# Decode attention of eight samples: three banks' worth of data taken out of a ring of four, and TensorE's work for a sample put in another order

## The reference, cut to what matters

```python
gate = einsum(q, mean of keys per block of 256)              # MoBA: top 3 blocks and the own one
o_a  = gathered_block_attn(q_a, k, v, idx, ..., 256)
ck = compress(k_cmp); cv = compress(v_cmp)                   # windows of 32, stride 16: gelu(flat @ w1 + b1) @ w2 + b2
p_cmp = softmax(q_b . ck);  o_cmp = p_cmp @ cv               # NSA, compressed branch
imp = p_cmp @ overlap;  idx = top_k(imp, 16)                 # which blocks of 64 the selected branch reads
o_sel = gathered_block_attn(q_b, k_sel, v_sel, idx, ..., 64)
o_win = window_attn(q_b, last 512 and own keys)
```

## Time and profile before

| | us |
|---|---|
| median of 3 runs (lowest, highest) | 1169.08 (1166.57, 1170.09) |
| the profiled execution, its own time | 1166.52 |
| its span, from first to last instruction | 1164.7 |
| TensorE busy in the span | 1017.6 (87%) |
| VectorE, ScalarE busy | 595.3, 486.9 |

### The profile page before, as it was taken

How to read it: one execution, slowest core, us unless ns; L and a number is a source line. 1 busy time by engine, 2 the same in 40 slices (tenths; PEclk the granted TensorE clock), 3 DMA queues, 4 the chain that set the end, 5 groups by cost and what they waited for, 6 DMA issues and landing times. The chain is left out here.

```text
span 1164.7 us, 25938 instructions
## 1 busy us (share of the span) xinstructions
PE 1017.6 (87%) x9553; PEld 890.4 (76%) x9553; DVE 595.3 (51%) x1304; ACT 486.9 (42%) x982; POOL 83.0 (7%) x59
## 2 busy tenths in 40 slices
PE   7789986775788989888888888879999799999997
PEld 3578874555585868677776767668998799999997
DVE  1500015523675756565665757568547764455433
ACT  3312224733263635445363636263443354443223
POOL 1143410000000000001010000000000000000000
PEclk9789995857899998999999999988999899999999
DMA  9787767318567475756666574556574164443501
GB/s 328 211 301 246 245 239 247 150 50 300 180 203 253 154 257 166 256 169 239 208 218 235 175 260 161 172 165 172 167 233 146 37 217 145 144 144 145 181 0 46
DMA packets 132533, 220.17 MB, mean 189 GB/s; under 512 B 20948, under 2 KB 76753, under 8 KB 127682
## 3 DMA queue, kind: packets, MB, share of 16 engines
q1 hardware_dynamic: 127586, 185.79, 48.4%
q0 software_dynamic: 4896, 33.68, 8.2%
HBM read 210.99 MB, written 12.58 MB: 192 GB/s over the span
## 5 line engine op out<-in xcount | busy, mean ns | idle before, releaser
L1240 PE MATMUL ps<-t_XT,t_slab 128*128 128x128 f32 x1024 | 162.2, 302 | 27.8 <-DVE t_cv L1842 15.6
L1240 PEld LDWEIGHTS ps<-t_XT,t_slab 128*128 128x128 f32 x1024 | 144.4, 214 | 45.4 <-ACT t_PTs L1530 20.6
L103 PE MATMUL ps<-b_uH,b_slabH 128*128 128x320 f32 x480 | 150.7, 314 | 8.8 <-DVE b_uL L2402 5.3
L104 PE MATMUL ps<-b_uL,b_slabH 128*128 128x320 f32 x480 | 150.1, 313 | 0.0
L105 PE MATMUL ps<-b_uH,b_slabL 128*128 128x320 f32 x480 | 149.2, 311 | 0.0
L2290 DVE TENSOR_TENSOR b_slabL<-t_slab,b_slabH 128x2048 fp32r<-128x2048 f32 (+1 forms) x52 | 109.3, 2125 | 64.1 <-ACT b_slabH L2183 64.0
L2183 ACT ACTIVATE b_slabH<-t_slab 128x2048 fp32r<-128x2048 f32 (+1 forms) x52 | 92.3, 1783 | 94.5 <-PE ps L105 87.2
L103 PEld LDWEIGHTS ps<-b_uH,b_slabH 128*128 128x128 f32 x480 | 91.8, 191 | 10.3 <-issue 6.6
L104 PEld LDWEIGHTS ps<-b_uL,b_slabH 128*128 128x128 f32 x480 | 91.8, 191 | 0.0
L105 PEld LDWEIGHTS ps<-b_uH,b_slabL 128*128 128x128 f32 x480 | 91.7, 191 | 0.0
L1240 PE MATMUL ps<-t_XT,t_taps 128*128 128x128 f32 x512 | 87.5, 287 | 0.0
(11 more groups left out here) (396 smaller groups left out, 2025.2 us busy)
## 6 DMA issues: line engine op xcount, KB each, us to landing
t_Kr<-cache_moba_kv SPq DMA_DIRECT2D x132, 256.0 KB, 3.0
t_Vr<-cache_moba_kv SPq DMA_DIRECT2D x124, 256.0 KB, 4.8
t_slab<-w_ada SPq DMA_DIRECT2D x22, 1024.0 KB, 7.9
t_slab<-w_gu SPq DMA_DIRECT2D x22, 1024.0 KB, 5.3
t_slab<-w_in SPq DMA_DIRECT2D x17, 1024.0 KB, 5.7
t_slab<-w_down SPq DMA_DIRECT2D x11, 1024.0 KB, 5.0
t_slab<-cmp_w SPq DMA_DIRECT2D x2, 2048.0 KB
t_wkv<-cache_nsa_win SPq DMA_DIRECT2D x8, 512.0 KB, 3.3
```

The costliest lines, as they stand in the source:

```text
L103: pe.matmul(out, w_high, x_high, start=start, stop=False, **kw)
L104: pe.matmul(out, w_high, x_low, start=False, stop=False, **kw)
L1240: return pe.matmul(out[:, P * j:P * j + P], taps(w, j, lp)[:, P * ht:P * ht + P], XT[:, w, lp, j, :, :].rearrange("p v i -> p (v i)"), sta ...
```

## The change

1. The window keys' transposes go to `S_WIN`, the transposes of `pwin` go to `H0`; both leave the ring (`OFF_RING`), and two empty places (`RESTS`) are put in so that the number of jobs on the ring stays a multiple of four. The compressed scores go to `H0` in place of `ps[7]`.
2. On TensorE `key_scores` becomes the last step of a sample, after `selected_scores(1)` and `hidden_keys(3)`. `moba_values(2)`, `segments(2)`, `compressed_values`, `selected_scores(0)`, `compressed_products` and `selected_transposes(2)` change places. At a sample's start 9 products (not 4) come ahead of `compressed_keys`, and 5 (not 8) between the window scores and the group sum.
3. On VectorE three of the four `gate_sums` come together ahead of `take_keys(0)`; the maximum of the compressed scores comes ahead of the additions to the own scores; the maximum of the window scores comes after that of the selected ones; the 16 `turn_keys` are spread otherwise.
4. On ScalarE the exponential of the window scores follows that of the selected ones; `relay_quarter(1)` comes ahead of the eight MoBA exponentials; quarter 1's work comes ahead of gelu, staging the queries after `relay_quarter(2)`, and the copy of quarter 2's selected keys after the output copy.

No arithmetic is added or removed, nor any transfer.

```diff
-STEADY = (FRONT_JOBS + cmp_jobs(0) + sel_jobs(0) + P_JOBS + cmp_jobs(1) + sel_jobs(1) + [("values", 0, 0), ("cout", 0, 0)]
-          + cmp_jobs(2) + sel_jobs(2) + cmp_jobs(3) + sel_jobs(3) + [("final", 0, 0)] + KEY_JOBS)
+RESTS = [("rest", 0, 0), ("rest", 1, 0)]
+OFF_RING = ("win", "pwin")
+STEADY = (FRONT_JOBS + RESTS + cmp_jobs(0) + sel_jobs(0) + P_JOBS + cmp_jobs(1) + sel_jobs(1)
+          + cmp_jobs(2) + [("values", 0, 0), ("cout", 0, 0)] + sel_jobs(2) + cmp_jobs(3) + sel_jobs(3) + [("final", 0, 0)] + KEY_JOBS)
...
+    def bank_of(it, job):
+
+        if job[0] in OFF_RING:
+            return S_WIN if job[0] == "win" else H0
+        return ps[RING[on_ring(NSA_JOBS if it is None else jobs_of(it)).index(job) % 4]]
...
             def sequence(it, more):
-                bank = ring(it, ("win", 0, 0))
+                bank = bank_of(it, ("win", 0, 0))
+                pe.wait_ge(scores_taken, it * N_SCORE + 2)
...
-                hidden_values(it, 0, range(0, 4), False)
+                hidden_values(it, 0, range(0, 9), False)
...
+                pe.matmul(H0[0:64, 0:NCMP], qb[:, :], ckT[:, 0:NCMP], start=True, stop=True).then_inc(small_mm, 1)
+                wait_emptied(it, ("win", 0, 0))
+                pe.matmul(S_WIN[0:64, :], qb[:, :], KTw[:, :], start=True, stop=True).then_inc(scored, 1)
+                hidden_values(it, 0, range(9, 14), False)
+                pe.wait_ge(pc_ready, it + 1)
                 pe.wait_ge(small_taken, it * 3 + 1)
-                pe.matmul(ps[7][0:64, 0:NCMP], qb[:, :], ckT[:, 0:NCMP], start=True, stop=True).then_inc(small_mm, 1)
-                wait_emptied(it, ("win", 0, 0))
-                pe.wait_ge(scores_taken, it * N_SCORE + 2)
-                pe.matmul(S_WIN[0:64, :], qb[:, :], KTw[:, :], start=True, stop=True).then_inc(scored, 1)
-                hidden_values(it, 0, range(4, 12), False)
-                pe.wait_ge(pc_ready, it + 1)
...
-                hidden_values(it, 0, range(12, 24), True)
+                hidden_values(it, 0, range(14, 24), True)
...
-                bank = ring(it, ("pwin", 0, 0))
+                bank = bank_of(it, ("pwin", 0, 0))
+                pe.wait_ge(exp_done, it * N_EXP + E_WIN)
...
+                moba_values(it, 2)
+                hidden_keys(it, it + 1, 1)
+                segments(2)
                 compressed_values(it)
-                hidden_keys(it, it + 1, 1)
+                selected_scores(it, it + 1, 0)
                 compressed_products(it)
-                moba_values(it, 2)
-                segments(2)
-                selected_scores(it, it + 1, 0)
-                selected_transposes(it, it + 1, 2)
                 hidden_keys(it, it + 1, 2)
                 moba_values(it, 3)
                 moba_own_values(it)
+                selected_transposes(it, it + 1, 2)
                 segments(3)
                 selected_transposes(it, it + 1, 3)
                 final_transposes(it)
-                key_scores(it, it + 1)
                 selected_scores(it, it + 1, 1)
                 hidden_keys(it, it + 1, 3)
+                key_scores(it, it + 1)
...
         def _(act):
...
                 act.wait_ge(max_done, it * N_MAX + 2)
-                exp(Sw[:, :], Sw[:, :], t["nmax"][:, 1:2], t["sums"][:, 1:2]).then_inc(exp_done, 1)
+                exp(Ss[:, :], Ss[:, :], t["sstat"][:, 0:1], t["sstat"][:, 1:2]).then_inc(exp_done, 1)
                 act.wait_ge(max_done, it * N_MAX + 3)
-                exp(Ss[:, :], Ss[:, :], t["sstat"][:, 0:1], t["sstat"][:, 1:2]).then_inc(exp_done, 1)
+                exp(Sw[:, :], Sw[:, :], t["nmax"][:, 1:2], t["sums"][:, 1:2]).then_inc(exp_done, 1)
...
                     odd_segments(it, 0, 1)
+                    relay_quarter(it, it + 1, 1)
...
-                if more:
-                    relay_quarter(it, it + 1, 1)
                 for q in (1, 3):
                     probability_copy(act, copy, it, q).then_inc(emptied_act, 1)
+                if more:
+                    keep_quarter(1)
+                    odd_segments(it, 1, 0)
+                    odd_segments(it, 1, 1)
+                    take_transposed_selected(it, 1)
                 act.wait_ge(hid_added, it * N_ADDED + 4)
                 gelu(1, 0)
                 gelu(1, 1).then_inc(cmp_act, 1)
                 if more:
+                    relay_quarter(it, it + 1, 2)
+                    keep_quarter(2)
                     stage_queries(it + 1)
                     pad_queries(it + 1)
-                    keep_quarter(1)
-                    odd_segments(it, 1, 0)
-                    odd_segments(it, 1, 1)
-                    take_transposed_selected(it, 1)
-                    relay_quarter(it, it + 1, 2)
-                    keep_quarter(2)
                     odd_segments(it, 2, 0)
                     odd_segments(it, 2, 1)
-                    take_transposed_selected(it, 2)
                     relay_quarter(it, it + 1, 3)
...
         def _(dve):
...
+                for i in range(3):
+                    gate_sums(it, i)
                 take_keys(it, 0)
-                dve.wait_ge(small_mm, it * N_SMALL + 1)
+                dve.wait_ge(small_mm, it * N_SMALL + 2)
+                dve.tensor_reduce(t["nmax"][:, 0:1], H0[0:64, 0:NCMP], AX.X, ALU.max, negate=True).then_inc(max_done, 1)
...
                 own_copy()
                 if more:
-                    turn_keys(it + 1, range(2, 6))
+                    turn_keys(it + 1, range(1, 4))
                     segment_differences(it, 1, 0)
                     segment_differences(it, 1, 1)
-                    values_copy()
-                    turn_keys(it + 1, range(6, 8))
-                    products_copy()
-                    turn_keys(it + 1, range(8, 12))
+                    turn_keys(it + 1, range(4, 8))
                     segment_differences(it, 2, 0)
                     segment_differences(it, 2, 1)
+                    values_copy()
                     take_selected(it + 1, 0)
-                    turn_keys(it + 1, range(12, 16))
+                    products_copy()
+                    turn_keys(it + 1, range(8, 14))
                     segment_differences(it, 3, 0)
                     segment_differences(it, 3, 1)
+                    turn_keys(it + 1, range(14, 16))
```

More of the change, by code:

```diff
@@ L983, with counted, on_ring @@
 P_JOBS = [("pmoba", q, 0) for q in range(4)] + [("pown", 0, 0)]
-STEADY = (FRONT_JOBS + cmp_jobs(0) + sel_jobs(0) + P_JOBS + cmp_jobs(1) + sel_jobs(1) + [("values", 0, 0), ("cout", 0, 0)]
-          + cmp_jobs(2) + sel_jobs(2) + cmp_jobs(3) + sel_jobs(3) + [("final", 0, 0)] + KEY_JOBS)
-LAST = FRONT_JOBS + P_JOBS + [("values", 0, 0), ("cout", 0, 0), ("final", 0, 0)]
+RESTS = [("rest", 0, 0), ("rest", 1, 0)]
+OFF_RING = ("win", "pwin")
+STEADY = (FRONT_JOBS + RESTS + cmp_jobs(0) + sel_jobs(0) + P_JOBS + cmp_jobs(1) + sel_jobs(1)
+          + cmp_jobs(2) + [("values", 0, 0), ("cout", 0, 0)] + sel_jobs(2) + cmp_jobs(3) + sel_jobs(3) + [("final", 0, 0)] + KEY_JOBS)
+LAST = FRONT_JOBS + RESTS + P_JOBS + [("values", 0, 0), ("cout", 0, 0), ("final", 0, 0)]
 RING = (0, 1, 2, 3)
-assert len(STEADY) % 4 == len(NSA_JOBS) % 4 == 0
 BY_DVE = KEY_JOBS + [("values", 0, 0), ("cout", 0, 0), ("pown", 0, 0), ("final", 0, 0), ("pmoba", 0, 0), ("pmoba", 2, 0)]
-N_RING = len(STEADY)
+def counted(jobs):
+    return [job for job in jobs if job[0] != "rest"]
+def on_ring(jobs):
+    return [job for job in jobs if job[0] not in OFF_RING]
+assert len(on_ring(STEADY)) % 4 == len(on_ring(NSA_JOBS)) % 4 == 0
+N_RING = len(counted(STEADY))
 N_SCORE, N_SMALL, N_ACT_CMP, N_OUT, N_EXP, N_MAX, N_HIDDEN, N_ADDED, N_STAGED = 3, 4, 4, 2, 7, 4, 3, 4, 6
@@ L1002, in by_act @@
 def by_act(jobs):
-    return [job for job in jobs if job not in BY_DVE]
+    return [job for job in counted(jobs) if job not in BY_DVE]
 PRO_DVE, PRO_ACT = len(by_dve(NSA_JOBS)), len(by_act(NSA_JOBS))
@@ L1199, in ring @@
             def ring(it, job):
-                jobs = NSA_JOBS if it is None else jobs_of(it)
+                jobs = on_ring(NSA_JOBS if it is None else jobs_of(it))
                 i = jobs.index(job)
-                if i >= 4:
+                if i >= 4 and jobs[i - 4] not in RESTS:
                     wait_emptied(it, jobs[i - 4])
                 elif it is not None:
-                    pe.wait_ge(*keys_emptied(it, i))
-                return ps[RING[i % 4]]
+                    pe.wait_ge(*keys_emptied(it, i % 4))
+                return bank_of(it, job)
             def segment_transposes(it, b, q, i):
@@ L1597, in sequence @@
                 act.wait_ge(filled, nth(it, ("win", 0, 0)))
-                copy(KTw[:, :], ps[RING[jobs_of(it).index(("win", 0, 0)) % 4]][:, :]).then_inc(emptied_act, 1)
+                copy(KTw[:, :], bank_of(it, ("win", 0, 0))[:, :]).then_inc(emptied_act, 1)
                 act.wait_ge(keys_mm, it + 1)
@@ L1614, in sequence @@
                     copy(PTs[:, 4 * n:4 * n + 4, :].rearrange("p l r -> p (l r)"),
```

(19 more changed lines are left out.)

36 lines of the change are left out of this document (14 added, 22 removed).

## The result

The changed kernel takes 1093.91 us (median of 4 runs, 1091.5 to 1095.42) against 1167.82 (4 runs) for the kernel before: 0.9364 of its time, 95% interval 0.9338 to 0.9389. The forecast was 1094, range 1080 to 1118. The profiled execution took 1091.5 us, its span 1089.7.

What follows compares the result with a forecast made beforehand. TensorE, nearest to full, was taken as the bound: 50.2 us work plus 1.9 waits, 52.1 a sample for 61.8, saves 68 over seven; with the ends 73.5, 1166.5 becomes 1093, profile-to-median allowance makes 1094, range 1080 to 1118.

Steps and rivals of the forecast that it cites:

- Floor of the work: TensorE's work in a sample without waits at full clock: 61.5 - 8.1 of waits - 3.2 of low clock = 50.2 us.
- Start of a sample: Waits of 2.23 and 0.75 us go; 5 products before the group sum cost nothing, by a cover of 0.3 us.
- Rival 2: A change of tables costs more than its own row: waits at group sum and `hidden_keys(2)`, 1110 us, chance 0.03.
- Group sum to `hidden_keys(0)`: VectorE's list ends at +12.1 us, subtractions at +13.5; 0.4 to 0.5 of `pwin`'s 1.20 us wait comes back.
- Last quarter of `probabilities`: ScalarE's MoBA exponentials end at +18.1 us, TensorE arrives at +17.6: 0.5 us of new wait.
- Quarters 1 and 2: Wait before `hidden_keys(1)` falls from 2.21 us to zero, within 0.3; at quarter 2 0.9 us replaces 0.70.
- rivals 1 and 5: 1: VectorE's and ScalarE's lists cost more, 1115 us, chance 0.10. 5: `take_keys` waits only move, 1140 us, chance 0.06.
- rival 6: More than forecast: the waits shrink to nothing, 50.2 us a sample, 1081 us, chance 0.08.
- The four terms: TensorE's waits: 0.45 us before `hidden_keys(0)`, 0.5 at `probabilities`, zero within 0.3 before `hidden_keys(1)`, 0.9 at quarter 2.
- Rivals 3 and 4: 3: short waits keep the clock low, 1117 us, chance 0.08. 4: clock low for long, slower than before, chance 0.03.
- Transfers: Quarter 3's gather lands about 3 us before `segments(3)`, costing nothing; without that cover ScalarE waits up to 1 us.
- Ends: Outside the seven-sample loop: 3.50 us go before the first sample, 2 us in the last one.

Runs made afterwards that it cites:

- both: Changed kernel with gelu ahead of quarter 1's segments on ScalarE, `keep_quarter(1)` later, and VectorE's fourth gate sum ahead of `take_keys(0)`: 1090.23 us.
- Experiment 1: Changed kernel with the window keys' transposes back on a ring bank, waiting for VectorE's taking of quarter 0: 1129.99 us.
- four_gates: Changed kernel with VectorE's fourth gate sum moved ahead of `take_keys(0)` with the other three: 1091.29 us.
- experiment 2: Changed kernel with the transposes of `pwin` back on ring bank 3, waiting for VectorE's taking of quarter 3: 1113.76 us.
- gelu_first: Changed kernel with ScalarE's gelu ahead of quarter 1's segments and `keep_quarter(1)` behind the copy of the selected keys: 1093.69 us.
- experiment 4: Changed kernel with `key_scores` ahead of `selected_scores(1)` and `hidden_keys(3)` again: 1116.64 us.
- experiments 7 to 10: Changed kernel rerun (1093.58 us) beside `gelu_first`, `four_gates` and `both`; then `both` with ScalarE's `relay_quarter(1)` behind the MoBA exponentials again: 1090.85 us.
- experiments 3 and 5: 3: `pwin` on ring bank 3, fourth gate sum ahead of `take_keys(0)`, 1097.07 us. 5: changed kernel, window transposes wait for VectorE's second gate sum, 1107.75 us.

## Why the prediction was right

- **Floor of the work, 50.2 us a sample.** TensorE's busy time is 50.25; `both`, with 0.43 of idle time shown, is at 50.9. Right.
- **Start of a sample.** No wait at the window transposes, the compressed scores or the group sum, and `key_scores` to compressed scores took 3.7 us (619.04 to 622.78) for my 3.6. Experiment 1 prices the bank of `win` at 36 us. The cover of 0.3 us before the group sum held: VectorE's scaling (L1774) ended at 624.99, TensorE started the group sum at 625.31. The exponential starts 0.02 us behind its table load (622.74 + 1.28, 624.04), and the load itself 0.01 behind the copy before it (622.36 + 0.37). The Trainium skill, ScalarE: Activation LUTs, section What ACT_TABLE_LOAD costs, adds a drain to a load; this trace doesn't show one. Rival 2 is out.
- **Group sum to `hidden_keys(0)`.** VectorE's list took +12.2 us and its subtractions +13.5, as laid out. The wait is 0.72 and not 0.45: TensorE started 0.35 us after the last subtraction, which I had not counted. `four_gates` shows that this list is the cause. That a part comes back shows in experiment 2: with 1.80 us of wait at `pwin` and none here, the sample with the clock up is 1.2 us longer than in the changed kernel, so 0.6 of the 1.80 is given back.
- **Last quarter of `probabilities`.** I had 0.5 us of wait, there is none. The exponentials ended at +17.8, not +18.1, and TensorE came 0.5 later (642.48 and three quarters of 1.92, +18.1 for my +17.6), most of it through the longer wait before. Two small errors of one direction; the term was 0.5 too large, 3.5 us in all, the largest miss of the sum.
- **Quarters 1 and 2.** Before `hidden_keys(1)` 0.30 (I had 0 to 0.3), before `compressed_products` 0.64 (0.9). `gelu_first` shows ScalarE's list with its table load as the cause of the second. That the 2.21 us before `hidden_keys(1)` went because quarter 1's work now comes ahead of gelu is read from the rows; no run puts that order back. Sum of waits 1.66 for 1.85, so rivals 1 and 5 are out; in rival 6 the waits would have gone.
- **Luck.** The four terms are off by +0.3, -0.5, +0.3 and -0.3 us and all but cancel. Before the loop 1.5 us more went than I said, behind it 0.8 less, and the median stands 2.4 us above the profiled execution, of which I took 1.3. That the forecast of 1094 meets 1093.91 is luck; that a sample comes out at 52.0 for 52.1 is so in part.
- **`key_scores` last.** The 1.02 us before it are gone; with the rest of the new order its old place would cost 2.23 us and the clock, 23 us (experiment 4). It does not free the start of a sample: the banks do.
- **The clock.** 1.00 in the loop. In the sample of the earlier trace rows it is worth 3.1 us (53.38 to 50.25 of TensorE's time) for my 3.2, on the mean of the seven 3.5. Rivals 3 and 4 are out: three waits of 0.30 to 0.72 us a sample started no low stretch in seven samples. The short idle times that keep the clock swinging by the Trainium skill, TensorE: Matmul & The Clock Gate, section A second HAM failure mode: psum-queue depth-cycling, come frequently; that section gives no length and no number, so these three a sample neither bear it out nor refute it.
- **Transfers.** Quarter 3's gather made ScalarE wait 1.32 us (655.17) in the sample shown and 0.96 to 3.78 us in the seven, for my "up to 1", and TensorE not at all. The longest of these ended 2.9 us before `segments(3)`, so the cover of 3 us was right. In experiments 7 to 10 quarter 2's gather, which I hadn't costed, does reach TensorE in some samples.
- **Ends.** Before the loop 5.0 us for my 3.5, but the front alone differs by as much between profiles; behind it 1.2 for 2: in the last sample the wait moved to `probabilities` (2.00 us at 691.53), and the clock fell behind it (0.86 from 680 to 720 us).

## What to carry to other kernels

A list of engine work in order of time, with each wait's releaser, is enough to lay out a new order by hand: keep apart what a wait costs, what comes back because the next list is just as late, and what the low clock behind it costs. A ring of banks orders jobs that have nothing to do with one another; a job whose bank holds an unrelated result that is read late should get a bank from outside. When the last waits are short, look for idle time of the releasing engine just before, and fill it with what stands in its way behind: the two edits of `both` do only that.

## What the runs showed of the hardware

The price of an idle time of TensorE is not in proportion to its length. In the seven samples of the loop, behind 1.21 and 1.38 us (experiments 3 and 5) the clock stayed at 2.4 GHz in every sample; behind 1.80 us it fell to 1.2 GHz in six of seven, behind 1.98 in three of seven, behind 2.23 (experiment 4) in five of seven, behind 2.81 in all. A fall cost 1.3 to 1.8 us of a sample, once 2.6 (experiment 4), over the wait itself. Why equal idle times of 1.8 to 2.2 us let it fall in one sample and not in the next stays open: nothing in TensorE's rows ahead of them differs, and 1.98 us at one place let it fall less often than 1.80 at another.

Two traces warn against taking 1.4 us for a safe length and 1.8 us for the full price. In the kernel before, the wait of 2.22 us in the first sample let the clock stay up, and behind the 2.23 us at the start of the second it stayed low for some 10 us, where in the sample of the earlier trace rows it was up again after some 3.5. This makes most of the 4.6 us by which the second sample is longer than the first; 16 instructions of L1240 take 3.79 us in it, where they take 2.05 in the sample of the earlier trace rows:

```profile
346.47 0.71 PE L1240 MATMUL ps<-t_XT,t_slab 128*128 128x128 f32 x4 [2.22 <-DVE t_cv L1842]
...
371.88 0.65 PE L1385 MATMUL ps<-t_ident,t_wkv 128*128 128x128 f32 x4 [2.23 <-DVE t_XT L1730]
...
378.99 3.79 PE L1240 MATMUL ps<-t_XT,t_slab 128*128 128x128 f32 x16
```

```profile
344.00:348.00 4.00, 1.78 (x16) 1.65 (x16) 2.82 (x7) 3.02 (x7) 0.94 (x1) 1.00 0.77 217
...
376.00:380.00 4.00, 3.33 (x8) 1.73 (x9) 1.98 (x9) 1.10 (x3) 0.00 (x0) 0.50 0.68 214
```

And in the last sample of `both`, 1.40 us with 0.35 us more behind the next four transposes were enough; the twelve that follow take 3.05 us. In `four_gates` the same two waits left the clock up.

```profile
687.56 0.63 PE L1370 MATMUL ps<-t_ident,t_XT 128*128 128x128 f32 x4 [1.40 <-ACT t_XT L1598]
688.54 3.05 PE L1370 MATMUL ps<-t_ident,t_XT 128*128 128x128 f32 x12 [0.35 <-ACT t_XT L1598]
```
